# Another order at the joints of a two-layer decoder step: staggered first pair of the mixing, P1 and P2 of the third FFN unit moved ahead

## The chip, the cores and the metric

One core of one Trainium2 chip. The metric is the device time of one execution of the whole program in microseconds; lower is better. The engines named here are TensorE (PE), VectorE (DVE), ScalarE (ACT), GpSimd (POOL) and SyncE (SP), which issues the loads. Each runs its own list of instructions in order and waits on semaphores.

## What is computed

The reference is one inference step of a decoder with two layers. 512 prompt tokens and 64 sample tokens go through with the same weights, in float32; the model width is 1024, that of the feed-forward network (FFN) 2816. Per layer:

```python
x = LN1(ALPHA * x + 0.5 * swiglu(x, ffn1_w_gate, ffn1_w_up, ffn1_w_down))
h = x @ w_in                      # pool input | q | k | v | cross q | 3 branch gates
y = (causal pooling, sliding-window attention with sinks, cross-attention into 256 memory tokens)
merged = sum(sigmoid(gate_b) * (y_b @ w_br_b) for b in range(3))
x = LN2(ALPHA * x + merged @ w_o)
x = LN3(ALPHA * x + 0.5 * swiglu(x, ffn2_w_gate, ffn2_w_up, ffn2_w_down))
```

The text calls everything between LN1 and LN2 the mixing. Outputs are x and the new caches.

## The kernel before, in words

**Numbers.** x lies transposed in SBUF: eight chunks (c) of 128 channels, each with 576 tokens in two halves (h) of 288. A matmul takes 128 x 128 weights and 288 tokens. Each float32 operand is split in a rounded part and its rest ("hi" and "lo"); `mm3` does three matmuls: hi x hi, hi x lo, lo x hi. ScalarE makes the rounded parts (`fill`, `round_w`, `round_x`, `round_sums`, `round_hidden`), VectorE or GpSimd the rests (`rest_of_sum`, `rest_w`, `rest_of_x`, `rest_of_sums`, `rest_of_hidden` on VectorE; `rest_of_quarter` and half of the mixing's chunks on GpSimd).

**FFN units.** Four FFNs run in a step, numbered fb 0 to 3 (two per layer). Most of an FFN is a list of units u (gate and up columns of a 128-column block, kind "G", or part of the down product, kind "D"), each by a fast 2x2 scheme with seven products P1 to P7 instead of eight; it needs sums of weight quarters (`first_sums`, `second_sum`, `third_sum` on VectorE) and sums of x (`sums_of_x`, for the four pairs i of chunks). A product of a G unit is 12 matmuls. P1, P2 and P4 take weight quarters as they are, rounded by ScalarE and GpSimd; P5, P6, P7 and P3 take sums. P1 and P2 take x itself, P5, P6, P7, P3, P4 sums of x (only the third unit has to wait for these, pair by pair, L1764 on: `xt_lo`). P1, P6, P7 and P4 accumulate one after the other in one PSUM bank; between them ScalarE copies it out: P1's value to another bank (`copy_p1`), P6's to u2 (L768), P7's to u3 (L739).

**The head.** The first two units (g = 0, 1) are done plainly: for each half h, unit g and w (gate, up) a product of 24 matmuls, so eight of them. `silu` and `head_hidden` turn them into hidden values; `hidden_sums` adds these up to forms, `round_hidden` and `rest_of_hidden` split the forms. The head begins while the layer norm before it still works: TensorE takes chunk after chunk as it is normalised (`round_x`, `finish_x` add the bias on ScalarE). Then comes the third unit, u = 2 (`HEADS`): P1, P5, P6, P2, P7.

**Order.** Every engine's order is written out by hand. `RUN` is that of TensorE's products, `HIGH` that of ScalarE's roundings, `LOW` and `LOW_POOL` those of the rests. On ScalarE the head is followed by `ffn`, for u = 2: copy_p1, round_hidden(0, 1), fill of P1 of u = 3, P4 and P3 of u = 2, `fill_a21` of u = 3, then the copy to u2. `fill_a21(3)` (L641) waits for VectorE's `rest_of_sum(2, "P3")`, which follows `rest_of_hidden(0, 1)` there. `SLOT` gives each product its place in the weight buffers; the head's and the tail's blocks use these places by number (`HEAD_SLOT`, `TAIL_SLOT`), and `fill` of the third unit waits until the head's product that had the place is done.

**The tail and the norms.** The last part of the down product is eight products p per half (`tail`), in pairs w, each pair added to x by `tail_sums` (L1194) and, from w = 1 on, into the sum for the mean (L1198). Half 1 of the tail runs while half 0 is normalised: `mean`, `center` (L1205), squares, `variance` (L1707), root, reciprocal, `scale` (L1214), rounding, rest. After FFN 1 of a layer `norm_plain` leads to `project_first`, which does the first two 128-column blocks s = 0, 1 of w_in in pair buffers 0 and 1; it has to wait for the tail's sums of these buffers, w = 2 and 3. Half 0 goes chunk by chunk through both blocks; in half 1 block 1 lags four chunks behind. After FFN 2 of layer 0 `norm_head(0, 2)` leads to the head of FFN 1 of layer 1. Mean and variance of half 1 are put between TensorE's products of the next part.

TensorE's order for the third unit and the wait of its P7 (for G units `read` is the count of ScalarE's copies from the bank, so P7 waits for the copy of P6's result to u2):

```python
RUN += [(HEADS, p) for p in ("P1", "P5", "P6", "P2", "P7")]
...
                elif prod == "P7":
                    pe.wait_ge(read, count - 1)
```

Of the kernel before, what the change touches and what calls it, by code (L numbers as in the profile page):

```python
# [7 lines left out]
ALU = mybir.AluOpType  # L8
# [4 lines left out]
P = 128  # L13
D = 1024
KC = D // P
# [4 lines left out]
TH = T // 2  # L20
# [62 lines left out]
RUN += [(HEADS, p) for p in ("P1", "P5", "P6", "P2", "P7")]  # L83
HIGH += [(HEADS, p) for p in ("P1", "P5", "P2", "P6", "P7")]
# [80 lines left out]
def build(nc, wblk, wg, wd, wt_d, x0, mem0, cst_d, par_d, mks_d, mvs_d, kcs_d, vcs_d, sps_d,  # L165
          y_out, kT_out, v_out, poolp_out, pools_out, mk_out, mv_out, kc_out, vc_out):
    with ExitStack() as ctx:
# [414 lines left out]
        def _(act):  # L582
# [99 lines left out]

            def head(fb):
# [27 lines left out]
                silu(1, 1)  # L711
                fill(fb, HEADS, "P6")
                fill(fb, HEADS, "P7")

            def ffn(fb):
                for u in range(HEADS, FU + 1):
# [5 lines left out]

                    def copy_p1():

                        act.wait_ge(f_done, done(fb, u, "P1"))
                        act.wait_ge(ep_set, 1)
                        if old:
                            act.wait_ge(c11_silu, g_count(fb, u - 1))
                        elif u > HEADS:
                            act.wait_ge(ep_free, d_count(fb, u - 1))  # L730
                        nc.scalar.activation(ep, al[u % 2], ACT.Copy).then_inc(p1_copied, 1)
# [68 lines left out]
            def round_x(l, n, h):  # L800

                for c in range(KC):
# [3 lines left out]
                    if (h, c) == (0, 3):  # L806
                        fill_head(2 * l + n, 0, 3)

# [8 lines left out]
            def norm_plain(l):  # L817
                prime(ACT.Sqrt)
                for h in range(2):
                    square(l, 0, h)  # L820
                    root(l, 0, h)
                    for c in range(KC):
# [7 lines left out]
                        if h == 0 and c in (3, KC - 1):  # L830

                            s = c // 4
# [154 lines left out]
        def _(dve):  # L987
# [107 lines left out]
            def head(fb):  # L1095
# [3 lines left out]
                for i in range(2):  # L1099
                    sums_of_x(fb, i)  # L1100
# [15 lines left out]
                rest_of_sum(fb, HEADS, "P7")  # L1116
                rest_of_hidden(fb, 0, 1)
# [72 lines left out]
            def tail_sums(fb, w, h):  # L1190
# [4 lines left out]
                if w > 0:  # L1195
                    dve.drain()
                    acc = two(lnsum[:, :])
                    nc.vector.tensor_tensor(acc, x[:, 0:2, half(h)] if w == 1 else acc, xw, ALU.add)  # L1198
                if w == KC // 2 - 1:
                    dve.drain().then_inc(sum_ready, 1)  # L1200

# [21 lines left out]
            def norm_plain(l):  # L1223
# [15 lines left out]
                for c in range(KC):  # L1239
# [21 lines left out]
            def norm_head(l, n):  # L1261
# [30 lines left out]
                for c in range(KC):  # L1292
# [5 lines left out]
                    if n == 2 and c == 5:  # L1298
                        tail_sums(fb - 1, 2, 1)
                rest_of_x(0, KC - 1)  # L1300
                if n == 2:
                    tail_sums(fb - 1, 3, 1)
# [311 lines left out]
        def _(pe):  # L1614
# [585 lines left out]
```

## Time and profile before

| | |
|---|---|
| median of 3 runs | 2574.58 us (2572.22 to 2579.29) |
| the profiled execution | 2574.16 us, span 2572.1 us |
| instructions | 45262 |
| VectorE busy | 1646.3 us (64%) |
| ScalarE busy | 1236.4 us (48%) |
| GpSimd busy | 608.6 us (24%) |
| mean DMA rate | 86 GB/s |
| mean granted TensorE clock | 0.975 of full speed |

The busy times are unions over the span of one execution. TensorE's share stands with the other rows below. A share says how much an engine does, not who sets the end of a stretch; for that the timelines of the engines are read side by side in the stretch. The times in a timeline are microseconds from the span's start. The four heads end at about 89, 939, 1348 and 2197 us; the first pair of the mixing is at 444 to 480 and 1703 to 1739 us, and the joint of the two layers at 1278 to 1320 us.

### The profile page before, as it was taken

The numbers are of one execution on the slowest core, as the hardware profiler recorded it, in microseconds if no ns is written. First come the engines' busy times: TensorE is split into PE (matmuls) and PEld (weight loads), VectorE is DVE, ScalarE is ACT, GpSimd is POOL, SyncE is SP. The second block draws the span as 40 slices with busy tenths as digits, with TensorE's granted clock in tenths as the row PEclk, the third lists the DMA queues.
The fourth block names the chain that finished last, engine by engine and source line by source line (L and its number), as shares of the span: only waits on it lengthen the run. The fifth ranks groups of instructions, "written<-read, shape, count | busy, mean of one in ns | idle before, by whom it ended". The sixth has DMA issues, their size and how long they took to land.

```text
span 2572.1 us, 45262 instructions
## 1 busy us (share of the span) xinstructions
PE 2446.5 (95%) x17636; PEld 2379.9 (93%) x17636; DVE 1646.3 (64%) x2752; ACT 1236.4 (48%) x2487; POOL 608.6 (24%) x540
## 2 busy tenths in 40 slices
PE   7999998899999989999989999989999998999997
PEld 6899998899999889999979999979999997999997
DVE  3878776435444587777587777664443447777775
ACT  4555554334422365655456556542343226655654
POOL 1333333120000123333423333321200001333332
PEclk9999999989999999999999999989899999999999
DMA  6132223221122212222213222323122221232221
GB/s 221 62 119 83 99 89 112 67 79 50 58 81 75 83 66 85 89 93 97 99 36 114 99 99 75 107 84 107 42 55 68 80 74 66 75 107 83 94 103 54
DMA packets 53523, 220.62 MB, mean 86 GB/s; under 512 B 15521, under 2 KB 18465, under 8 KB 40225
## 3 DMA queue, kind: packets, MB, share of 16 engines
q1 hardware_dynamic: 53312, 217.74, 24.9%
q8 instruction: 142, 2.33, 0.4%
q14 instruction: 69, 0.56, 0.1%
HBM read 213.64 MB, written 6.04 MB: 85 GB/s over the span
## 4 chain that ended last, share of the span: by engine, by line
PE 80%; DVE 12%; ACT 4%; DVEq 2%; issue 1%; DMA 0%; ACTq 0%; POOL 0%
PE pair L1769 13%; PE pair L1771 12%; PE pair L1770 12%; PE pair L1618 9%; PE pair L1620 9%; PE pair L1622 9%; PE S L1769 2%; PE S L1771 2%; PE S L1770 2%; PE S L1707 2%; DVE htl L1085 2%; DVE TP L1005 1%; ACT hth L652 1%; PE S L1864 1%; PE TP L1924 1%
## 5 line engine op out<-in xcount | busy, mean ns | idle before, releaser
L1769 PE MATMUL pair<-xth,hiA 128*128 128x288 f32 x1280 | 382.4, 299 | 23.8 <-POOL loA L1532 12.5
L1770 PE MATMUL pair<-xtl,hiA 128*128 128x288 f32 x1280 | 380.9, 298 | 0.0
L1771 PE MATMUL pair<-xth,loA 128*128 128x288 f32 x1280 | 380.5, 297 | 0.0
L606 ACT ACTIVATE hiA<-TP 128x512 fp32r<-128x512 f32 (+1 forms) x384 | 200.6, 556 | 213.3 <-DVE TP L1010 141.9
L1618 PE MATMUL pair<-xh,hiA 128*128 128x288 f32 x1088 | 255.4, 312 | 26.1 <-DVE x L1194 15.8
L1532 POOL TENSOR_TENSOR loB<-rawB,hiB 128x512 fp32r<-128x512 f32 (+1 forms) x128 | 159.6, 1248 | 490.7 <-ACT hiB L606 490.7
L991 DVE TENSOR_TENSOR loA<-rawA,hiA 128x1024 fp32r<-128x1024 f32 x108 | 134.1, 1241 | 219.9 <-ACT hiA L593 219.3
L1769 PEld LDWEIGHTS pair<-xth,hiA 128*128 128x128 f32 x1280 | 242.9, 190 | 27.7 <-POOL loA L1532 13.4
L996 DVE TENSOR_TENSOR loA<-TP,hiA 128x512 fp32r<-128x512 f32 (+1 forms) x384 | 244.2, 636 | 29.6 <-ACT hiA L606 27.1
L1620 PE MATMUL pair<-xl,hiA 128*128 128x288 f32 x1088 | 244.3, 302 | 0.0
L1622 PE MATMUL pair<-xh,loA 128*128 128x288 f32 x1088 | 244.0, 302 | 0.0
L1771 PEld LDWEIGHTS pair<-xth,loA 128*128 128x128 f32 x1280 | 243.7, 190 | 0.0
L1770 PEld LDWEIGHTS pair<-xtl,hiA 128*128 128x128 f32 x1280 | 243.4, 190 | 0.0
L1532 POOL TENSOR_TENSOR loB<-rawA,hiB 128x512 fp32r<-128x512 f32 (+1 forms) x128 | 153.1, 1196 | 343.6 <-ACT hiB L606 343.6
L1618 PEld LDWEIGHTS pair<-xh,hiA 128*128 128x128 f32 x1088 | 183.2, 195 | 37.8 <-DVE loA L991 18.3
L1769 PE MATMUL pair<-xth,hiB 128*128 128x288 f32 x640 | 191.9, 300 | 14.0 <-DVE c L1142 10.1
L1770 PE MATMUL pair<-xtl,hiB 128*128 128x288 f32 x640 | 189.0, 295 | 0.0
L1771 PE MATMUL pair<-xth,loB 128*128 128x288 f32 x640 | 188.3, 294 | 0.0
L1620 PEld LDWEIGHTS pair<-xl,hiA 128*128 128x128 f32 x1088 | 183.7, 195 | 0.2
L1622 PEld LDWEIGHTS pair<-xh,loA 128*128 128x128 f32 x1088 | 182.9, 195 | 0.0
L593 ACT ACTIVATE hiA<-rawA 128x1024 fp32r<-128x1024 f32 x108 | 113.8, 1053 | 139.4 <-PE TP L1622 80.5
L1769 PE MATMUL pair<-hth,hiA 128*128 128x288 f32 x576 | 172.2, 299 | 1.7 <-DVE x L1128 1.6
(322 smaller groups left out, 6702.1 us busy)
## 6 DMA issues: line engine op xcount, KB each, us to landing
rawA<-in_wblk SPq DMA_DIRECT2D x108, 512.0 KB, 3.4
rawB<-in_wg SPq DMA_DIRECT2D x44, 1024.0 KB, 4.8
rawA<-in_wg SPq DMA_DIRECT2D x44, 1024.0 KB, 4.8
rawB<-in_wd SPq DMA_DIRECT2D x24, 768.0 KB, 4.1
rawA<-in_wd SPq DMA_DIRECT2D x24, 768.0 KB, 4.4
rawA<-in_wt_d SPq DMA_DIRECT2D x4, 1024.0 KB, 4.7
rawB<-in_wt_d SPq DMA_DIRECT2D x4, 1024.0 KB, 4.8
mcs<-in_mks SPq DMA_DIRECT2D x2, 2048.0 KB, 9.8
```

Source lines behind the costliest of these rows:

```text
L593: nc.scalar.activation(wh[:, s, :], raw[:, s, :], ACT.Copy).then_inc(w_hi, 1)
L606: nc.scalar.activation(slot((hiA, hiB), prod, n), src, ACT.Copy).then_inc(f_hi, 1)
L991: nc.vector.tensor_tensor(wl[:, s, :], raw[:, s, :], wh[:, s, :].bitcast(F32), ALU.subtract).then_inc(w_lo, 1)
L996: nc.vector.tensor_tensor(slot((loA, loB), prod, n), sum_bank(prod, n), slot((hiA, hiB), prod, n).bitcast(F32), ALU.subtract).then_inc(f_l ...
L1085: nc.vector.tensor_tensor(htl[:, n % 3, forms, :], hf[:, forms, :], hth[:, n % 3, forms, :].bitcast(F32), ALU.subtract).then_inc(h_lo, 1)
L1532: nc.gpsimd.tensor_tensor(slot((loA, loB), prod, n), quarter(u, prod, n), slot((hiA, hiB), prod, n).bitcast(F32), ALU.subtract).then_inc(f ...
L1618: nc.tensor.matmul(out(h), wt[0], xt[0](h), start=(kk == 0), stop=False)
L1620: nc.tensor.matmul(out(h), wt[0], xt[1](h), start=False, stop=False)
L1622: last = nc.tensor.matmul(out(h), wt[1], xt[0](h), start=False, stop=(kk == nk - 1))
L1769: nc.tensor.matmul(bank, wt_hi, xt[0], start=start, stop=False, skip_group_check=True)
L1770: nc.tensor.matmul(bank, wt_hi, xt[1], start=False, stop=False, skip_group_check=True)
L1771: last = nc.tensor.matmul(bank, wt_lo, xt[0], start=False, stop=i == n - 1, skip_group_check=True)
```

## The change

It changes orders and waits, and no computation.

- `RUN`: the third unit's P1 goes ahead of the head's last product; behind that come P2, P5, P6, P7. TensorE's `head` walks through `RUN` and does P1 itself. `SLOT` swaps the places of P1 and P2, so that P1's place is one that the head's first unit leaves.
- ScalarE in `head`: P1's fill moves up behind `silu(0, 1)`, then `copy_p1`, P2 and P5; `round_hidden(fb, 0, 0)` moves from behind `round_sums(1)` to the end; `round_sums(3)` moves behind P6 and P7. `finish_x` of chunks 0 to 3 is done within `round_x`.
- VectorE in `head`: `second_sum`, the rests of P6 and P7 and `third_sum` come ahead of all work on the hidden values.
- `project_first`: half 0 gets the same lag of four chunks as half 1; block 0 waits for its own weights and tail sum alone; `variance` comes behind all of half 0.
- `norm_plain` and `norm_head`: `tail_sums` is split in `tail_onto_x` (to x, which TensorE waits for) and `tail_into_mean`; the first comes earlier, the second later. `round_w` and `rest_w` of block 0 come earlier.
- The head of FFN 1 of layer 1 has mean and variance one product later, as the other heads have them.

```diff
-SLOT = {"P1": 0, "P6": 1, "P5": 2, "P7": 3, "P2": 4, "P4": 5, "P3": 6}
+SLOT = {"P2": 0, "P6": 1, "P5": 2, "P7": 3, "P1": 4, "P4": 5, "P3": 6}
-TAIL_SLOT = [(EXTRA, 0, 2, 1, 3, 4, 5, 6), (4, EXTRA, 5, 6, 0, 2, 1, 3)]
+TAIL_SLOT = [(EXTRA, 2, 1, 3, 0, 4, 5, 6), (4, EXTRA, 5, 6, 0, 2, 1, 3)]
-RUN += [(HEADS, p) for p in ("P1", "P5", "P6", "P2", "P7")]
-HIGH += [(HEADS, p) for p in ("P1", "P5", "P2", "P6", "P7")]
+RUN[-1:] = [(HEADS, "P1"), RUN[-1]] + [(HEADS, p) for p in ("P2", "P5", "P6", "P7")]
+HIGH += [(HEADS, p) for p in ("P1", "P2", "P5", "P6", "P7")]
...
@@ ScalarE, head
                 if fb:
-                    for c in range(KC):
+                    for c in range(4, KC):
                         finish_x(l, n, 1, c)
                 round_sums(fb, 0)
                 silu(0, 1)
+                fill(fb, HEADS, "P1")
                 round_sums(fb, 1)
-                round_hidden(fb, 0, 0)
+                copy_p1(fb, HEADS)
+                fill(fb, HEADS, "P2")
+                fill(fb, HEADS, "P5")
                 round_sums(fb, 2)
-                fill(fb, HEADS, "P1")
-                fill(fb, HEADS, "P5")
-                round_sums(fb, 3)
-                fill(fb, HEADS, "P2")
                 silu(1, 1)
                 fill(fb, HEADS, "P6")
                 fill(fb, HEADS, "P7")
+                round_sums(fb, 3)
+                round_hidden(fb, 0, 0)
...
@@ ScalarE, ffn
-                    if on:
-                        copy_p1()
                     if u == HEADS:
                         round_hidden(fb, 0, 1)
                     elif on:
+                        copy_p1(fb, u)
                         fill(fb, u, "P2")
...
@@ ScalarE, round_x
+                    if h == 1 and c >= 4:
+                        finish_x(l, n, 1, c - 4)
...
@@ ScalarE, norm_plain
-                        if h == 0 and c in (3, KC - 1):
-                            s = c // 4
+                        if h == 0 and c in (1, 3):
+                            s = c // 2
...
@@ VectorE, head
                 first_sums(fb, HEADS)
-                for i in range(2):
-                    sums_of_x(fb, i)
+                sums_of_x(fb, 0)
+                sums_of_x(fb, 1)
                 rest_of_sums(fb, 0)
                 sums_of_x(fb, 2)
                 head_hidden(fb, 0, 1)
-                hidden_sums(fb, 0)
                 rest_of_sums(fb, 1)
-                sums_of_x(fb, 3)
-                rest_of_hidden(fb, 0, 0)
-                rest_of_sums(fb, 2)
                 rest_of_sum(fb, HEADS, "P5")
                 second_sum(fb, HEADS)
-                rest_of_sums(fb, 3)
-                head_hidden(fb, 1, 1)
-                hidden_sums(fb, 1)
+                sums_of_x(fb, 3)
+                rest_of_sums(fb, 2)
                 rest_of_sum(fb, HEADS, "P6")
                 third_sum(fb, HEADS)
                 rest_of_sum(fb, HEADS, "P7")
+                rest_of_sums(fb, 3)
+                hidden_sums(fb, 0)
+                head_hidden(fb, 1, 1)
+                rest_of_hidden(fb, 0, 0)
+                hidden_sums(fb, 1)
                 rest_of_hidden(fb, 0, 1)
...
@@ VectorE, norm_plain (norm_head with n == 2: onto_x of pair 2 at c == 4, the rest alike)
-                    if c == 5:
-                        tail_sums(fb, 2, 1)
-                rest_w(pq(l, Q_IN), 0)
+                    if c == 3:
+                        rest_w(pq(l, Q_IN), 0)
+                        tail_onto_x(fb, 2, 1)
                 rest_of_x(0, KC - 1)
+                tail_onto_x(fb, 3, 1)
                 rest_w(pq(l, Q_IN), 1)
-                tail_sums(fb, 3, 1)
+                tail_into_mean(2, 1)
+                tail_into_mean(3, 1)
...
@@ TensorE, project_first
-                begin(qq, 0, u)
-                begin(qq, 1, u)
-                for w in range(2, 4):
-                    pe.wait_ge(tail_add, tail_count(2 * l, w, 1))
...
+                for h in range(2):
+                    turns = [(c, 0) for c in range(lag)] + [(c - lag * s, s) for c in range(lag, KC) for s in range(2)]
+                    for c, s in turns + [(c, 1) for c in range(KC - lag, KC)]:
+                        if h == 0 and c == 0:
+                            begin(qq, s, u)
+                            pe.wait_ge(tail_add, tail_count(2 * l, 2 + s, 1))
...
-                    if (h, c, s) == (0, 6, 1):
+                        if (h, c, s) == (0, KC - 1, 1):
...
@@ TensorE, head
+                for _, g, w, h in [what for what in RUN if what[0] == "H"]:
...
+                    if (g, w, h) == (1, 1, 1):
+                        product(fb, HEADS, "P1")
...
+                        if fb and (h, c) == (0, 3) and (g, w) == (0, 1):
+                            mean(l, n, 1)
+                        if fb and (h, c) == (0, 3) and (g, w) == (1, 0):
+                            variance(l, n, 1)
```

## Rows read from the trace of the kernel before

**Rows 1.** the page, part 1: engine, busy us, share of span, instructions

```profile
PE 2446.5 (95%) x17636; PEld 2379.9 (93%) x17636; DVE 1646.3 (64%) x2752; ACT 1236.4 (48%) x2487; POOL 608.6 (24%) x540
```

**Rows 2.** waits of TensorE, 905 to 945 us: us, times, longest

```profile
PE pair L1769 <- POOL loA L1532: 3.6, 1, 3.6
PE pair L1769 <- DVE loA L996: 1.2, 1, 1.2
```

**Rows 3.** timeline of VectorE, 912 to 939 us: start, us, instruction

```profile
913.88 1.23 DVE L1005 TENSOR_TENSOR TP<-S,rawA 128x1024 f32<-128x1024 f32 x1
...
921.92 0.46 DVE L1032 TENSOR_TENSOR tf<-x,tf 128x288 f32<-128x288 f32 x1
...
926.38 1.36 DVE L1032 TENSOR_TENSOR tf<-x,tf 128x288 f32<-128x288 f32 x1
...
929.80 0.68 DVE L996 TENSOR_TENSOR loA<-TP,hiA 128x512 fp32r<-128x512 f32 x1
...
932.27 0.45 DVE L1092 SCALAR_TENSOR_TENSOR hf<-c,pair 128x288 f32<-128x288 f32 x1
...
933.63 0.46 DVE L1076 TENSOR_TENSOR hf<-hf 128x288 f32<-128x288 f32 x1
934.01 0.68 DVE L996 TENSOR_TENSOR loA<-TP,hiA 128x512 fp32r<-128x512 f32 x1
...
935.81 1.65 DVE L1085 TENSOR_TENSOR htl<-hf,hth 128x1440 fp32r<-128x1440 f32 x1
...
938.78 1.23 DVE L1005 TENSOR_TENSOR TP<-S,rawB 128x1024 f32<-128x1024 f32 x1 [0.73 <-ACT S L641]
```

**Rows 4.** timeline of ScalarE, 912 to 942 us

```profile
913.77 3.50 ACT L814 ACTIVATE x<-x,par 128x288 f32<-128x288 f32 x8
...
923.62 0.68 ACT L652 ACTIVATE hth<-hf 128x576 fp32r<-128x576 f32 x1 [3.46 <-DVE hf L1071]
...
934.13 1.41 ACT L652 ACTIVATE hth<-hf 128x1440 fp32r<-128x1440 f32 x1 [1.55 <-DVE hf L1076]
...
938.15 0.60 ACT L641 ACTIVATE S<-rawB 128x512 f32<-128x512 f32 x1 [1.09 <-DVE loB L996]
938.69 0.39 ACT L768 ACTIVATE u<-pair 128x288 f32<-128x288 f32 x1
```

**Rows 5.** timeline of TensorE, 923 to 940 us

```profile
927.48 0.61 PE L1769 MATMUL pair<-xth,hiA 128*128 128x288 f32 x1 [3.60 <-POOL loA L1532]
...
939.18 0.37 PE L1769 MATMUL pair<-xth,hiA 128*128 128x288 f32 x1 [0.98 <-issue]
```

**Rows 6.** timeline of GpSimd, 912 to 942 us

```profile
925.95 1.48 POOL L1532 TENSOR_TENSOR loA<-rawA,hiA 128x512 fp32r<-128x512 f32 x1 [21.09 <-ACT hiA L606]
929.57 1.45 POOL L1532 TENSOR_TENSOR loB<-rawA,hiB 128x512 fp32r<-128x512 f32 x1 [2.14 <-ACT hiB L606]
```

**Rows 7.** windows: length, busy us per engine, granted clock, DMA share

```profile
448.35:455.18 6.83, 3.19 (x13) 3.21 (x14) 4.04 (x5) 1.47 (x3) 0.97 (x1) 0.50 0.50 156
926.22:933.05 6.83, 5.57 (x22) 5.42 (x23) 6.54 (x9) 3.51 (x7) 2.66 (x2) 0.50 0.00 0
```

**Rows 8.** timeline of TensorE, 440 to 480 us

```profile
452.00 0.58 PE L1618 MATMUL pair<-xh,hiA 128*128 128x288 f32 x1 [7.89 <-DVE x L1194]
```

**Rows 9.** timeline of VectorE, 434 to 455 us

```profile
442.40 0.94 DVE L1214 SCALAR_TENSOR_TENSOR x<-x,par,lnstd 128x288 f32<-128x288 f32 x2
...
449.85 1.22 DVE L991 TENSOR_TENSOR loA<-rawA,hiA 128x1024 fp32r<-128x1024 f32 x1
451.00 0.75 DVE L1194 TENSOR_TENSOR x<-x,pair 128x576 f32<-128x576 f32 x1
```

**Rows 10.** timeline of VectorE, 1286 to 1306 us

```profile
1295.98 0.74 DVE L1194 TENSOR_TENSOR x<-x,pair 128x576 f32<-128x576 f32 x1
...
1303.90 2.27 DVE L1205 TENSOR_TENSOR x<-x,TP 128x288 f32<-128x288 f32 x6 [2.41 <-PE TP L1700]
```

More of the change, by code:

```diff
@@ L681, in prime, with copy_p1 @@
                 nc.scalar.activation(small[:, 60:61], small[:, 61:62], function)
+            def copy_p1(fb, u):
+                act.wait_ge(f_done, done(fb, u, "P1"))
+                act.wait_ge(ep_set, 1)
+                if u > HEADS:
+                    if SEQ[u - 1][0] == "G":
+                        act.wait_ge(c11_silu, g_count(fb, u - 1))
+                    else:
+                        act.wait_ge(ep_free, d_count(fb, u - 1))
+                nc.scalar.activation(ep, al[u % 2], ACT.Copy).then_inc(p1_copied, 1)
             def head(fb):
@@ L721, in ffn @@
                     groups = H_GROUPS[j_old // 2] if old else []
[L723 to L731, printed above, removed]
                     def fill_next(prod):
@@ L1188, in ffn, with tail_onto_x @@
                     tail_sums(fb, w, 0)
-            def tail_sums(fb, w, h):
+            def tail_onto_x(fb, w, h):
                 dve.wait_ge(f_done, done(fb, "T", 2 * w + 1, h))
@@ L1194, in tail_sums, with tail_into_mean @@
                 nc.vector.tensor_tensor(xw, xw, halves(pair[w % 2]), ALU.add).then_inc(tail_add, 1)
[L1195 to L1198, printed above, removed]
+            def tail_into_mean(w, h):
+                dve.drain()
+                acc = two(lnsum[:, :])
+                nc.vector.tensor_tensor(acc, x[:, 0:2, half(h)] if w == 1 else acc, x[:, 2 * w:2 * w + 2, half(h)], ALU.add)
                 if w == KC // 2 - 1:
                     dve.drain().then_inc(sum_ready, 1)
+            def tail_sums(fb, w, h):
+                tail_onto_x(fb, w, h)
+                if w > 0:
+                    tail_into_mean(w, h)
             def center(l, n, h):
@@ L1297, in norm_head @@
                         tail_sums(fb - 1, 1, 1)
-                    if n == 2 and c == 5:
-                        tail_sums(fb - 1, 2, 1)
+                    if n == 2 and c == 4:
+                        tail_onto_x(fb - 1, 2, 1)
                 rest_of_x(0, KC - 1)
                 if n == 2:
-                    tail_sums(fb - 1, 3, 1)
+                    tail_onto_x(fb - 1, 3, 1)
+                    tail_into_mean(2, 1)
+                    tail_into_mean(3, 1)
                 else:
@@ new lines, in head @@
+                l, n = ((fb - 1) // 2, 2 - f) if fb else (None, None)
+                for _, g, w, h in [what for what in RUN if what[0] == "H"]:
+                    if h == 1:
+                        pe.wait_ge(head_out if w else head_silu, head_count(fb, g, 0))
+                    elif f == 1 and g == 1:
+                        pe.wait_ge(pair_free[w], n_use(fb // 2, Q_WO + 3) + 2)
+                    elif f == 0 and fb > 0:
+                        pe.wait_ge(tail_add, tail_count(fb - 1, 2 + w, 1))
+                    if (g, w, h) == (1, 1, 1):
+                        product(fb, HEADS, "P1")
+                    for c in range(KC):
+                        q_no = 2 * w + c % 2
+                        if h == 0 and c < 2:
+                            pe.wait_ge(f_lo_p, lo_p_count(fb, "H", g, q_no))
+                        if g == 0 and w == 0:
+                            pe.wait_ge(xf_lo, x_count(fb, h, c))
+                        cols = slice(c // 2 * P, c // 2 * P + P)
+                        last = mm3(lambda _: (al, de)[w][g], [head_slot(f, part, g, q_no)[:, cols] for part in range(2)],
+                                   [lambda _, t=t: x_form(t, h, c) for t in ((xth, xbh), (xtl, xbl))], c, KC, (h,))
+                        if fb and (h, c) == (0, 3) and (g, w) == (0, 1):
+                            mean(l, n, 1)
+                        if fb and (h, c) == (0, 3) and (g, w) == (1, 0):
+                            variance(l, n, 1)
+                    last.then_inc(f_done, 1)
@@ L1834, in ffn @@
                 for what in RUN:
-                    if what[0] not in ("H", "T"):
+                    if what[0] not in ("H", "T") and what != (HEADS, "P1"):
                         product(fb, *what)
```

45 lines of the change are left out of this document (8 added, 37 removed).

## The prediction

> **What bounds the kernel now.** I read the page first: the matmul row is busy 95% of the span [rows 1], so there is little to win, and only where TensorE stands still. TensorE's waits over a head's end (905 to 945 us) name 3.6 us for GpSimd's rounding of the third unit's P1 and 1.2 us for VectorE's rounding of a sum [rows 2]; a third, 0.98 us, ends at P7 [rows 5]. "Third unit" is u = 2, HEADS. Is it really those products that set the end of this stretch? VectorE's timeline says no. From `first_sums` at 913.88 on it is never idle for longer than a drain until the rounding of P3 is done: the first real idle is the 0.73 us before 938.78, so 24.2 us, to 938.05, are without a hole [rows 3]. ScalarE goes on from there: a21 of the next unit at 938.15, then the copy of P6's result (u2, L768) at 938.69 [rows 4], and P7, which accumulates on the same bank, starts at 939.18 [rows 5]. So a head ends when a VectorE chain ends, 25.3 us after `first_sums`; the 3.6 us of idle TensorE lies beside that chain and costs nothing. After P7 TensorE runs without such a stop. The program has four heads of this form.
>
> **Step 1, the head (four times).** P1 goes ahead of the head's last product and P2 ahead of P5. That moves 2 x 12 matmuls to an earlier place and removes none. It can gain only if VectorE's chain gets shorter. Its operations are the same, in another order, so I look for the idle that the order makes.
> (a) Before, between `hidden_sums(1)` (its last operation starts at 933.63) and the rounding of its result (935.81) VectorE does three operations (P6's rounding, the third sum, P7's rounding), which fill the 1.80 us from 934.01 on [rows 3]. They cover ScalarE's `round_hidden(0, 1)`, 1.41 us from 934.13 [rows 4]. After, these three stand ahead of `hidden_sums(0)`, and nothing lies between: VectorE waits the 1.41 us and a handing over of some 0.07. The same happens once more, smaller, at `round_hidden(0, 0)`: 0.68 us [rows 4], of which `head_hidden(1, 1)`, 0.45 at 932.27 [rows 3], hides a part: 0.37 stay, with hand-overs. Sum 1.85 us. `fill(3, "P1")`, P4, P3, a21 and the u2 copy are all queued on ScalarE behind `round_hidden(0, 1)`, and P7 behind them, as before.
> (b) `finish_x` of chunks 0 to 3 moves in between the rounds of x. Eight of them take 3.50 us now [rows 4], 0.43 each; three fit into ScalarE's holes between the rounds of x, which follow VectorE's pace, and the last one stands ahead of `silu(1, 0)` and a21, for which `first_sums` waits: 0.4 us later. Not in head 0, which has no such step. That ScalarE is 1.7 us freer afterwards gains nothing, since its `round_sums(0)` waits for VectorE's sums.
> (c) GpSimd's roundings of P1 and P2, and VectorE. Before, P1's at 925.95 met VectorE's L1032 at 926.38, which took 1.36 us instead of the 0.46 of the same line at 921.92; P2's at 929.57 met one that reads PSUM (929.80), which took no more than its like at 934.01, 0.68 [rows 3, 6]. After, P1's weights are rounded at about 919.4 and P2's at 923.6, both among the sums of x, which are SBUF only: two delays of 0.9 against one, +0.9.
> On this the Trainium skill (SBUF — State Buffer, § SBUF: two separate sides) is sterner: a VectorE operation with two SBUF inputs and a GpSimd one that reads SBUF shut each other out for the whole instruction. By that rule each of the two delays could be the whole 1.45 us of such a rounding, and the sum below would be 4 x 1.1 higher, 2596.0 us. The rows agree that the second waits, but the 0.9 is what this trace shows of it.
> Sum: 1.85 + 0.9 = 2.75 in head 0, 3.15 in the other three: 12.2 us. Bounds for a head: 1.5 (a alone, the smaller part hidden) and 4.0 (P1 rounded late, so that the last product too stands behind it).
>
> **Step 2, TensorE's clock behind the head.** A matmul took 3.19 / 13 = 0.245 us at the low level [rows 7], so some 0.13 at the high one: 1.6 us for a product of 12, 3.2 for one of the head's 24, 0.39 for a turn of three. P1, the last product and P2 now follow each other (6.4 us); then P5 needs rounded sums 3 and 4 of x, which VectorE gives at about 931.2 and 934.3. P6 ends at about 936.5, and P7 starts at 939.18 + 3.15 = 942.3: some 6 us of idle TensorE at the very end of the chain, where 0.98 were [rows 5]. After 7.9 us of idle before 452.00 the granted clock was 0.50, the 1.2 GHz level, from 448.35 to 455.18, so 3.2 us of it fell on work; after 3.6 us before 927.48 it was 0.50 until 933.05, 5.6 us of it on work [rows 5, 7, 8]. That second one costs nothing now, since VectorE's chain is longer. After the change the low level reaches past P7, where TensorE is the bound: half of the mean of 3.2 and 5.6 is 2.2 us, four times 8.8. Bounds: 0 (the level stays, as a shorter idle might allow), and half of the whole 6.83, 3.4, per head.
>
> **Step 3, the first pair of the mixing (two layers).** TensorE starts at 452.00 after 7.9 us of idle, when the last tail sum has been added (VectorE, 451.00 to 451.75) [rows 8, 9]. After, block 0 needs only its own weights and the third pair sum: rest_w(0) moves up behind chunk 2 (442.4, where the scales of chunks 4 and 5 now start, + 1.22, its duration at 449.85) [rows 9], `tail_onto_x(2, 1)` ends at about 444.4, and TensorE runs five turns, to 446.5. Then block 1's weights come: VectorE does four scales, two rests, the last `onto`, then rest_w(1): about 451.0. So 4.9 us of idle are left of 7.9. But the remaining turns now run at 0.50 for longer: before, 3.19 us of work fell on the low level [rows 7]; now a low stretch that begins some 3 us later takes in up to 6.8, 1.8 us lost; and the last two turns (0.8 us) come ahead of the variance instead of behind it. 3.0 - 1.8 - 0.8 = 0.4. If the stretch begins where it did, 2 us. I take 1.0 per layer, 2.0 together. Bounds: 0 and 4.6 (mean 3.1 us earlier and both low stretches gone). The sums `into` the mean follow rest_w(1) and end at 452.8, before TensorE reaches the mean; the earlier round_w(0) on ScalarE stands in its wait for chunk 2 and delays nobody. SP's loads have their waits unchanged.
>
> **Step 4, the joint of the two layers (once).** The pair sum that TensorE waits for is added from 1295.98 to 1296.72 [rows 10]; it moves to about 1294.2, behind chunk 4. Mean comes one product later but without its low clock: the centring, now at 1303.90 [rows 10], would start at 1302.4, and the variance chain ends about 1.6 us earlier. From there the head of step 1 follows: 1.6 us gained. Bounds 0 and 3.2.
> Slots of P1 and P2 swap numbers; each has its slot to itself within the units, and the tail's fills wait for products long done: nothing. The last norm is untouched.
>
> **The sum.** 12.2 + 8.8 - 2.0 - 1.6 = +17.4 us. The profiled execution took 2574.16 us with a span of 2572.1, against a median of 2574.58 (2572.22 to 2579.29), so it stands for the median within 0.5 us. 2574.2 + 17.4 = 2591.6. A measurement can tell 0.3%, 7.7 us: faster is below 2566.5, slower above 2582.
>
> **Rivals.**
> A. TensorE is the bound at the heads after all (faster). Mechanism: in the joint of the mixing, work put into the idle keeps the clock at 2.4 GHz and each layer's joint gives 4.6 us; in the heads the new holes on VectorE are covered by something I take as waiting. Point of decision: P7 of unit 2 starts no later than 25.3 us after `first_sums`. For it: TensorE did wait 3.6 us for P1 and 8 us for the tail sum. Against: VectorE without a hole. 2574.2 - 9.2 - 1.6 = 2563.4. Chance 0.14.
> B. The heads lose their 12.2 us, but the clock stays up past P7, and the other joints give all, 9.2 + 1.6: 2574.2 + 12.2 - 10.8 = 2575.6, no change that can be told. For: five turns in the hole at 444. Against: every idle of over 3 us read above was followed by 0.50. Chance 0.18.
> C. The change doesn't do what it says: P1's weights are late although asked for sooner, because ScalarE reaches the fill only behind `round_sums(0)` and `silu(0, 1)`, and GpSimd then waits for VectorE; P1 holds up the ready last product, and copy_p1 holds ScalarE's P2 and P5. 1.3 us more per head: 2591.6 + 5.2 = 2596.8. Chance 0.08.
> The forecast has 0.60. Its own range, by the bounds, is 2580 to 2604. The range for all goes from 2567 (into A's side) to 2603. Slower: C and nearly all of the forecast, 0.64; within 0.3%: B and the forecast's lower edge, 0.22; faster: A, 0.14.
>
> **What would show it.** In the changed trace: P7 (L1769, the first write of the pair bank after P6) starts 27.5 to 29 us after `first_sums` (25.3 before); VectorE idles some 1.5 us ahead of its 128x1440 rounding, waiting for ScalarE; P5 shows two stops for the rounded sums; the granted clock is 0.50 behind P7. In the mixing's joint: TensorE starts within 1 us of the tail's end, stops some 4.5 us for rest_w, and the mean comes about 1 us earlier. I am wrong if VectorE is idle less than 1 us between `first_sums` and P3's rounding, or if P7 follows P6 closely.

## The result, and the profile after

The changed kernel takes 2588.75 us (median of 5 runs, 2584.64 to 2590.36); the kernel before, run beside it, takes 2574.13 us (2571.70 to 2579.29). The ratio is 1.0052, with a 95% interval of 1.004 to 1.0064: slower by 0.52%, 13.4 us. The forecast was 2591.6 us. The profiled execution of the changed kernel took 2589.03 us with a span of 2587.0, so it stands for the median within 0.3 us, and can be compared with the forecast step by step.

Part 1 of the page has the same work in a span that is 14.9 us longer; only TensorE's busy time grew [rows 1], by 12.5 us for the same 17636 matmuls, and that is a slower clock, not more work:

```profile
PE 2459.0 (95%) x17636; PEld 2387.4 (92%) x17636; DVE 1646.4 (64%) x2752; ACT 1236.8 (48%) x2487; POOL 609.2 (24%) x540
```

**The head.** The waits of TensorE from 905 to 945 us no longer name GpSimd's rounding of P1 [rows 2]. The wait that the change was made against is gone, and another stands there:

```profile
PE pair L1780 <- DVE xtl L1041: 5.2, 2, 2.8
PE pair L1780 <- issue: 4.4, 2, 4.3
```

VectorE's timeline, which had no hole of over 0.2 us between `first_sums` and the rounding of P3 [rows 3], now has two, each ahead of a rest of hidden values and each ended by ScalarE's rounding of them (L652):

```profile
914.66 1.23 DVE L1008 TENSOR_TENSOR TP<-S,rawA 128x1024 f32<-128x1024 f32 x1
...
919.83 2.50 DVE L1041 TENSOR_TENSOR xtl<-tf,xth 128x1152 fp32r<-128x1152 f32 x1
...
924.88 1.81 DVE L1041 TENSOR_TENSOR xtl<-tf,xth 128x1152 fp32r<-128x1152 f32 x1
...
935.72 0.76 DVE L1088 TENSOR_TENSOR htl<-hf,hth 128x576 fp32r<-128x576 f32 x1 [0.39 <-ACT hth L652]
936.57 0.76 DVE L1077 TENSOR_TENSOR hf<-hf 128x576 f32<-128x576 f32 x1
937.40 0.46 DVE L1079 TENSOR_TENSOR hf<-hf 128x288 f32<-128x288 f32 x1
939.33 1.66 DVE L1088 TENSOR_TENSOR htl<-hf,hth 128x1440 fp32r<-128x1440 f32 x1 [1.47 <-ACT hth L652]
```

The holes are 0.39 and 1.47 us. ScalarE's rows are those of before [rows 4], only later: the rounding, a21, and the copy to u2, behind which P7 stands:

```profile
937.89 1.40 ACT L652 ACTIVATE hth<-hf 128x1440 fp32r<-128x1440 f32 x1 [2.21 <-DVE hf L1079]
...
941.68 0.60 ACT L641 ACTIVATE S<-rawB 128x512 f32<-128x512 f32 x1 [0.86 <-DVE loB L999]
942.22 0.39 ACT L769 ACTIVATE u<-pair 128x288 f32<-128x288 f32 x1
```

GpSimd's two roundings [rows 6] came forward. The first now begins together with VectorE's L1041 of 919.83:

```profile
919.82 1.29 POOL L1546 TENSOR_TENSOR loB<-rawA,hiB 128x512 fp32r<-128x512 f32 x1 [14.59 <-ACT hiB L606]
924.09 1.39 POOL L1546 TENSOR_TENSOR loA<-rawA,hiA 128x512 fp32r<-128x512 f32 x1 [2.97 <-ACT hiA L606]
```

TensorE's timeline has the two stops within P5, and then P7, 28.05 us after `first_sums` where it was 25.30 [rows 3, 5]:

```profile
927.67 0.29 PE L1780 MATMUL pair<-xth,hiA 128*128 128x288 f32 x1
...
931.41 0.41 PE L1780 MATMUL pair<-xth,hiA 128*128 128x288 f32 x1 [2.78 <-DVE xtl L1041]
...
934.47 0.61 PE L1780 MATMUL pair<-xth,hiA 128*128 128x288 f32 x1 [2.39 <-DVE xtl L1041]
...
942.71 0.58 PE L1780 MATMUL pair<-xth,hiA 128*128 128x288 f32 x1 [4.27 <-issue]
943.09 0.45 PE L1781 MATMUL pair<-xtl,hiA 128*128 128x288 f32 x1
943.33 0.45 PE L1782 MATMUL pair<-xth,loA 128*128 128x288 f32 x1
```

The last two rows start 0.24 us apart where a matmul at full clock takes 0.13: TensorE runs at the 1.2 GHz level behind P7. The granted clock in these windows shows it: the first lies in the mixing's first pair and answers to [rows 7], the second ahead of P7, the third at P7. (Behind the window and its length stand the busy us of TensorE, its weight loads, VectorE, ScalarE and GpSimd, then granted clock, DMA share and GB/s.)

```profile
454.20:461.00 6.80, 6.16 (x21) 5.59 (x22) 2.33 (x4) 0.00 (x0) 0.00 (x0) 0.50 0.25 77
...
932.10:938.90 6.80, 3.97 (x15) 3.62 (x15) 5.12 (x8) 1.69 (x2) 0.00 (x0) 0.50 0.00 0
942.30:945.70 3.40, 2.99 (x12) 3.02 (x13) 2.52 (x3) 1.21 (x3) 1.04 (x1) 0.50 0.41 82
```

**The mixing's first pair.** In TensorE's timeline the wait of 7.89 us [rows 8] has become one of 0.43 and one of 3.72, with five turns of three matmuls between them:

```profile
448.90 0.37 PE L1632 MATMUL pair<-xh,hiA 128*128 128x288 f32 x1 [0.43 <-DVE x L1197]
...
454.84 0.61 PE L1632 MATMUL pair<-xh,hiA 128*128 128x288 f32 x1 [3.72 <-DVE loA L994]
```

**Where the 14.9 us are.** I took the start of the same operations in both traces (P7 of each head, the mean and variance of each norm, the first product behind the first pair) and looked where the difference grows. In us:

| stretch | grows by (negative: shorter) | forecast |
|---|---|---|
| four heads, up to P7 | 2.55 + 2.18 + 2.80 + 2.28 = 9.8 | 12.2 |
| from P7 to the next mean (clock) | 1.86 + 1.33 + 2.66 + 2.76 = 8.6 | 8.8 |
| mixing, first pair, layers 0 and 1 | -1.91 - 3.58 = -5.5 | -2.0 |
| joint of the two layers | -2.33 | -1.6 |
| stretches that the diff doesn't touch | -1.15 + 2.5 + 2.96 = +4.3 | 0 |

The last line is two attention parts and the last norm. Their work is the same; low stretches of the clock lie elsewhere in them. From the last mean to the end it is 38.4 us here, with a granted clock of 0.50 from 2567.1 to 2573.9, and 35.4 both before and in the trace of the changed joints alone. So a single trace can carry some 3 us of this that no part of the diff explains. That is why each part was run by itself.

### The profile page after: what moved, and what is told of

Its sections match the earlier page's. It is cut to its first block, busy times and chain, and to the rows that moved or that the text cites. A ratio compares the mean times of both kernels' runs of the same rounds, so it can differ in the third digit from the quotient of the medians.

```text
span 2587.0 us, 45262 instructions
## 1 busy us (share of the span) xinstructions
PE 2459.0 (95%) x17636; PEld 2387.4 (92%) x17636; DVE 1646.4 (64%) x2752; ACT 1236.8 (48%) x2487; POOL 609.2 (24%) x540
## 3 DMA queue, kind: packets, MB, share of 16 engines
q8 instruction: 142, 2.33, 0.4%
## 4 chain that ended last, share of the span: by engine, by line
PE 79%; DVE 12%; ACT 5%; DVEq 2%; issue 1%; DMA 0%; POOL 0%; ACTq 0%
PE pair L1780 12%; PE pair L1782 12%; PE pair L1781 12%; PE pair L1632 9%; PE pair L1634 9%; PE pair L1636 9%; PE S L1718 2%; DVE htl L1088 2%; PE S L1780 2%; PE S L1782 2%; PE S L1781 2%; ACT hth L652 2%; DVE TP L1008 1%; PE S L1875 1%; PE TP L1935 1%
## 5 line engine op out<-in xcount | busy, mean ns | idle before, releaser
L1780 PE MATMUL pair<-xth,hiA 128*128 128x288 f32 x960 | 290.4, 303 | 35.2 <-DVE xtl L1041 17.9
L1780 PE MATMUL pair<-xth,hiB 128*128 128x288 f32 x960 | 287.5, 300 | 14.7 <-DVE c L1145 10.9
L1781 PE MATMUL pair<-xtl,hiA 128*128 128x288 f32 x960 | 288.9, 301 | 0.0
L1782 PE MATMUL pair<-xth,loA 128*128 128x288 f32 x960 | 288.2, 300 | 0.0
L1781 PE MATMUL pair<-xtl,hiB 128*128 128x288 f32 x960 | 284.6, 296 | 0.0
L1782 PE MATMUL pair<-xth,loB 128*128 128x288 f32 x960 | 283.9, 296 | 0.0
L1780 PEld LDWEIGHTS pair<-xth,hiA 128*128 128x128 f32 x960 | 185.0, 193 | 38.4 <-DVE xtl L1041 20.0
L1780 PEld LDWEIGHTS pair<-xth,hiB 128*128 128x128 f32 x960 | 181.6, 189 | 22.1 <-issue 20.4
L1546 POOL TENSOR_TENSOR loA<-rawB,hiA 128x512 fp32r<-128x512 f32 (+1 forms) x64 | 76.4, 1194 | 497.1 <-ACT hiA L606 497.1
L1782 PEld LDWEIGHTS pair<-xth,loB 128*128 128x128 f32 x960 | 181.9, 190 | 0.0
L1781 PEld LDWEIGHTS pair<-xtl,hiB 128*128 128x128 f32 x960 | 181.7, 189 | 0.0
## 6 DMA issues: line engine op xcount, KB each, us to landing
mcs<-in_mks SPq DMA_DIRECT2D x2, 2048.0 KB, 10.1
```

Source lines behind the costliest of these rows:

```text
L1546: nc.gpsimd.tensor_tensor(slot((loA, loB), prod, n), quarter(u, prod, n), slot((hiA, hiB), prod, n).bitcast(F32), ALU.subtract).then_inc(f ...
L1780: nc.tensor.matmul(bank, wt_hi, xt[0], start=start, stop=False, skip_group_check=True)
L1781: nc.tensor.matmul(bank, wt_hi, xt[1], start=False, stop=False, skip_group_check=True)
L1782: last = nc.tensor.matmul(bank, wt_lo, xt[0], start=False, stop=i == n - 1, skip_group_check=True)
```

## The experiments

Two sets, each timed against the kernel before on the same chip: the first four against a median of 2576.52 us, the last four against 2574.38 us.

### One half of the change at a time

`joints_only` has the heads of before (order, `SLOT`, ScalarE's and VectorE's `head`) and all the changed joints; `heads_only` is the other way round.

```diff
 joints_only, against the changed kernel
-RUN[-1:] = [(HEADS, "P1"), RUN[-1]] + [(HEADS, p) for p in ("P2", "P5", "P6", "P7")]
+RUN += [(HEADS, p) for p in ("P1", "P5", "P6", "P2", "P7")]
 heads_only, against the changed kernel
-                        if h == 0 and c in (1, 3):
-                            s = c // 2
+                        if h == 0 and c in (3, KC - 1):
+                            s = c // 4
...
```

> The changed joints (first pair of the mixing, joint of the two layers) on the heads of before. The forecast's steps 3 and 4 say 3.6 us faster than before (2570.5); the trace of the changed kernel, read against that of before, says some 6 (2568). Rival B says 9.2 + 1.6 = 10.8 us faster (2563). If the joints are worth nothing it is 2574.

> The changed heads on the joints of before. Forecast: steps 1 and 2, 12.2 + 8.8 = 21 us slower than before (2595), P7 of the third unit 28.05 us after first_sums in all heads. If only the longer chain of VectorE counts and the low clock behind it costs nothing: 12 us slower (2586). If TensorE is the bound at the heads (rival A): no slower than before.

Measured: joints_only 2567.23 us, ratio 0.9963 (0.995 to 0.9975); heads_only 2595.95 us, ratio 1.0077 (1.0063 to 1.0091). Against their shared before that is -9.3 and +19.4 us. So the change is a gain and a loss twice as large, added up (10.1 us, and 13.4 for the whole change, which the intervals allow). The heads cost what Steps 1 and 2 say (12.2 + 8.8 = 21.0; the interval is 16 to 23). The joints give more than the 3.6 of Steps 3 and 4; even the near end of the interval is 6.4.

In heads_only the hole and P7 are where they are in the changed kernel, P7 28.06 us after `first_sums` (919.76); in joints_only P7 comes after 25.6 to 26.3 us, near the 25.3 to 26.0 of the kernel before. VectorE's and TensorE's timelines of heads_only:

```profile
942.51 0.46 DVE L1079 TENSOR_TENSOR hf<-hf 128x288 f32<-128x288 f32 x1
944.44 1.66 DVE L1088 TENSOR_TENSOR htl<-hf,hth 128x1440 fp32r<-128x1440 f32 x1 [1.47 <-ACT hth L652]
```

```profile
947.82 0.58 PE L1772 MATMUL pair<-xth,hiA 128*128 128x288 f32 x1 [4.41 <-issue]
```

### Is it the clock behind the head?

`warm_heads` is the changed kernel with matmuls that nothing reads in TensorE's three waits of each head: 7 and 6 at the stops of P5, 15 ahead of P7 (these 15 take 5.84 us).

```diff
+            def warm(n):
+                for _ in range(n):
+                    nc.tensor.matmul(pair[1][:, 0, 288:512], ident, cst[:, 0:224], start=False, stop=True, skip_group_check=True)
...
+                if (u, prod) == (HEADS, "P7"):
+                    warm(15)
...
+                    if (u, prod) == (HEADS, "P5") and i >= 2:
+                        warm(9 - i)
```

> The changed kernel, with dummy matmuls of TensorE (identity times a constant into unused columns of P5's bank) where it stands still for P5's third and fourth pair and for P7: 7, 6 and 15 in each head. They keep the engine busy and wait for nothing; the outputs are the same. If the low clock behind the wait is a cost of its own (step 2), it goes: about 8.8 us faster than the changed kernel (2580), with P7 still 28.05 us behind first_sums and a granted clock of 1.0 behind it. If the low clock costs nothing, or the chain alone makes the loss: the same as the changed kernel, 2588.8. If the dummies hold up the real work, slower than it.

Measured: 2580.63 us, ratio 1.0018 (1.0008 to 1.0027), 8.7 us below the changed kernel's ratio. P7 starts 28.91, 27.83, 28.05 and 28.06 us after `first_sums` in the four heads, 0.45 us later in sum than in the changed kernel; in heads 0 and 1 it follows the unread matmuls without a wait. So what is gained is the clock. Windows over two heads, first of the changed kernel, then of warm_heads:

```profile
930.00:950.00 20.00, 11.93 (x63) 11.38 (x64) 14.76 (x20) 10.03 (x17) 4.91 (x4) 0.74 0.17 54
1340.00:1360.00 20.00, 11.64 (x50) 11.09 (x51) 14.73 (x20) 8.81 (x15) 3.44 (x2) 0.66 0.16 53
```

```profile
930.00:950.00 20.00, 20.00 (x131) 20.00 (x130) 14.66 (x23) 9.95 (x18) 6.92 (x5) 1.00 0.15 54
1340.00:1360.00 20.00, 19.43 (x125) 18.76 (x125) 15.14 (x23) 10.33 (x19) 7.04 (x5) 1.00 0.15 54
```

The 0.74 and 0.66 have become 1.00. From P7 to the next mean the four heads together take 8.6 us more than in the kernel before in the trace of the changed kernel, 9.2 in that of heads_only, and 0.6 in that of warm_heads. So Step 2's 8.8 us are shown as a cause, not only as a sum. A loss in VectorE's chain alone would have left the time where it was.

### Cover ScalarE's rounding again

`cover_round` keeps the changed head and gives VectorE back what lay behind each rounding: P6's rest behind `head_hidden(1, 1)`, the third sum and P7's rest behind `hidden_sums(1)`.

```diff
-                rest_of_sum(fb, HEADS, "P6")
-                third_sum(fb, HEADS)
-                rest_of_sum(fb, HEADS, "P7")
...
                 head_hidden(fb, 1, 1)
+                rest_of_sum(fb, HEADS, "P6")
                 rest_of_hidden(fb, 0, 0)
                 hidden_sums(fb, 1)
+                third_sum(fb, HEADS)
+                rest_of_sum(fb, HEADS, "P7")
                 rest_of_hidden(fb, 0, 1)
```

> The changed kernel, with VectorE's rounding of P6 put over ScalarE's round_hidden(0, 0), and third_sum and P7's rounding behind hidden_sums(1), over round_hidden(0, 1), where they stood before. Step 1a says that VectorE's two holes (0.39 and 1.47 us) are closed to some 0.3: the chain from first_sums to P7 goes from 28.05 to 26.5 us, 4 x 1.5 = 6 us faster than the changed kernel (2583). Rival: the loss comes from GpSimd and VectorE shutting each other out and from P1's place, then nothing moves.

Measured: 2581.36 us, ratio 1.002 (1.0011 to 1.0029). VectorE's timeline: the hole of 0.39 is gone, that of 1.47 is 0.27.

```profile
933.84 0.75 DVE L1088 TENSOR_TENSOR htl<-hf,hth 128x576 fp32r<-128x576 f32 x1
...
935.89 0.69 DVE L1018 TENSOR_TENSOR S<-rawA,TP 128x512 f32<-128x512 f32 x1
936.49 0.68 DVE L999 TENSOR_TENSOR loA<-TP,hiA 128x512 fp32r<-128x512 f32 x1
937.44 1.66 DVE L1088 TENSOR_TENSOR htl<-hf,hth 128x1440 fp32r<-128x1440 f32 x1 [0.27 <-ACT hth L652]
```

P7 follows `first_sums` by 26.60, 25.66, 26.38 and 26.38 us, where it was 28.27, 28.05, 28.04 and 28.04: 7.4 us sooner in all, and the ratio fell by 0.0032, 8.2 us. The holes are 1.59 us shorter, and in three heads P7 is 1.66 or 1.67 sooner: a hole of VectorE in the head is paid one for one, as (a) of Step 1 says. The further 0.7 us of head 1 come from the meeting of VectorE and GpSimd, which the next run brings up.

### The bias of x in its old place

`no_finish` takes `finish_x` of chunks 0 to 3 out of `round_x` again.

```diff
-                    for c in range(4, KC):
+                    for c in range(KC):
                         finish_x(l, n, 1, c)
...
-                    if h == 1 and c >= 4:
-                        finish_x(l, n, 1, c - 4)
```

> The changed kernel, with finish_x of chunks 0 to 3 behind silu(1, 0) and a21 again, not within round_x. Step 1b says 0.4 us a head in the three heads that have it: first_sums follows the reciprocal of its norm 0.4 us sooner, 1.2 us faster than the changed kernel in all, which is within the noise of the runs but can be read in the trace. Rival: sums_of_x then has to wait for finish_x and the gain is lost.

Measured: 2584.32 us, ratio 1.0035 (1.0023 to 1.0047), 4.4 us below the changed kernel; the two intervals overlap a little. The timeline of VectorE has `first_sums` (L1006) 0.79 us behind the start of the last rest of x, where the changed kernel has 1.20 and the kernel before 0.80: (b) of Step 1 is exactly its 0.4. But in these heads 1 to 3 P7, too, comes 27.33 or 27.34 us after `first_sums`, 0.7 sooner than the 28.05 of the changed kernel, which (b) alone would have left as it was. VectorE, then GpSimd, of no_finish:

```profile
914.72 0.52 DVE L1289 SCALAR_TENSOR_TENSOR xtl<-x,par,xth 128x288 fp32r<-128x288 f32 x1 [0.17 <-ACT xth L805]
...
915.51 1.23 DVE L1006 TENSOR_TENSOR TP<-S,rawA 128x1024 f32<-128x1024 f32 x1
...
920.67 1.36 DVE L1039 TENSOR_TENSOR xtl<-tf,xth 128x1152 fp32r<-128x1152 f32 x1
922.12 1.35 DVE L1028 TENSOR_TENSOR tf<-x 128x288 f32<-128x288 f32 x1
```

```profile
920.86 2.30 POOL L1544 TENSOR_TENSOR loB<-rawA,hiB 128x512 fp32r<-128x512 f32 x1 [14.37 <-ACT hiB L606]
```

Here VectorE's L1039 began 0.19 us before GpSimd's rounding, and GpSimd paid (2.30 for 1.29) while VectorE kept its 1.36 and lost 0.9 only in the next operation (1.35, where 0.45 is usual). In the changed kernel both began within 0.01 us, and VectorE paid there (2.50) and once more later (1.81), 1.6 in all. The 0.4 us of (b) move these two against each other, so that (b) and (c) are not independent, as I had them.

But the outcome can change without any edit. In head 1 of warm_heads and of cover_round, where VectorE's, ScalarE's and GpSimd's orders up to here are those of the changed kernel, GpSimd again begins 0.01 us ahead or at the same time, and this time GpSimd paid. ScalarE's copy to u2 came 0.7 us sooner behind `first_sums` for it than in heads 2 and 3. VectorE's rows and GpSimd's of warm_heads:

```profile
919.31 1.36 DVE L1041 TENSOR_TENSOR xtl<-tf,xth 128x1152 fp32r<-128x1152 f32 x1
920.76 1.34 DVE L1030 TENSOR_TENSOR tf<-x 128x288 f32<-128x288 f32 x1
919.30 2.48 POOL L1546 TENSOR_TENSOR loB<-rawA,hiB 128x512 fp32r<-128x512 f32 x1 [14.60 <-ACT hiB L606]
```

### The mixing alone

`mixing_only` is the kernel before with the first pair staggered: `project_first`, `rest_w` and `round_w` of block 0 earlier, `tail_sums` split in `norm_plain`.

```diff
                     if c == 3:
+                        rest_w(pq(l, Q_IN), 0)
+                        tail_onto_x(fb, 2, 1)
...
```

> Of the changed joints only the first pair of the mixing (two places); the joint of the two layers and the heads are those of before. Both joints together gave some 8 us. Step 3 says 1.0 us a layer (0 to 4.6), step 4 1.6 for the joint of the layers. If the traces of the changed kernel tell the shares rightly (1.9 and 3.6 us in the two layers, 1.6 at the joint of the layers), this one is 5.5 us faster than before, and joints_only 2 to 3 us faster still. If step 3 is right, only 2 us faster.

Measured: 2570.06 us, ratio 0.9983 (0.9974 to 0.9992), -4.4 us, where Step 3 says -2.0. By the same landmarks the first pair gives 3.4 us in layer 0 and 2.5 in layer 1 in this trace, 1.9 and 3.6 in that of the changed kernel: 2.9 in the mean. The other traces agree. From the mean to the first product behind the pair the old order takes 51.8 to 52.3 us (before and heads_only), the new one 48.4 to 49.9 (the seven traces that have it without unread matmuls in it), 2.9 less in the mean. The stops are the same in all of these seven. TensorE's timeline of mixing_only:

```profile
444.86 0.37 PE L1627 MATMUL pair<-xh,hiA 128*128 128x288 f32 x1 [0.44 <-DVE x L1194]
...
450.80 0.61 PE L1627 MATMUL pair<-xh,hiA 128*128 128x288 f32 x1 [3.72 <-DVE loA L991]
...
465.92 0.61 PE L1627 MATMUL pair<-xh,hiA 128*128 128x288 f32 x1 [4.30 <-DVE xl L1238]
```

### An earlier copy to u2

`u2_early` is joints_only with ScalarE's copy of P6's result put ahead of a21 of the next unit.

```diff
+                    if u == HEADS:
+                        act.wait_ge(f_done, done(fb, u, "P6"))
+                        nc.scalar.activation(u2[:, :], al[u % 2], ACT.Copy).then_inc(al_act, 1)
...
-                    if g:
+                    if g and u > HEADS:
```

> joints_only, with ScalarE's copy of P6's result to u2 ahead of fill_a21(3) in the third unit, so that P7 no longer hangs on VectorE's chain. If that queue place is what sets the end of a head, P7 starts some 1.1 us earlier behind first_sums (24.0 instead of 25.2), as soon as P2 is done, and the program is 2 to 4 us faster than joints_only (some 0.95 a head as far as the copy to u3 lets P4 start). If VectorE's chain binds TensorE at P3 or at the next unit anyway, P7 moves and the program does not get faster.

Measured: 2566.32 us, ratio 0.9967 (0.9955 to 0.998), against 0.9963 of joints_only: no gain that these intervals can tell. In the traces P7 starts 1.4 and 1.1 us sooner behind `first_sums` in heads 3 and 2, but not in heads 0 and 1 (26.2 and 25.9 us, where joints_only has 26.3 and 25.7): there it follows P2 without a wait in either run. In head 2, the only one where it waited in joints_only, it waits no more and starts 24.54 us after `first_sums` instead of 25.65. TensorE's timeline, joints_only and then u2_early:

```profile
1343.43 0.37 PE L1777 MATMUL pair<-xth,hiA 128*128 128x288 f32 x1 [0.97 <-issue]
...
1370.98 0.37 PE L1777 MATMUL pair<-xth,hiB 128*128 128x288 f32 x1 [0.15 <-DVE c L1142]
```

```profile
1341.79 0.29 PE L1780 MATMUL pair<-xth,hiA 128*128 128x288 f32 x1
...
1370.18 0.37 PE L1780 MATMUL pair<-xth,hiB 128*128 128x288 f32 x1 [0.84 <-DVE c L1145]
```

Of the 0.97 us that P7 no longer waits, 0.69 come back as a longer wait for VectorE one unit later. From `first_sums` to the next mean the four heads take 1459.1 us in joints_only and 1458.6 in u2_early. P7 is a landmark of VectorE's chain, and moving it without shortening the chain brought next to nothing.

### A version that beats both

`best` is u2_early with unread matmuls in the remaining waits of the joints, as in warm_heads: 9 and 11 at the two stops of the mixing's first pair, 5 ahead of the head of each FFN 2, 5 and 3 in the last norm.

```diff
+                        if (h, c, s) == (0, 0, 1):
+                            warm(pair[0][:, 0, :], 9)
+                        if (h, c, s) == (1, 0, 0):
+                            warm(pair[0][:, 0, :], 11)
...
```

> u2_early with dummy matmuls in TensorE's waits at the joints, as in warm_heads: 9 and 11 in the first pair of the mixing (ahead of block 1 of half 0 and ahead of half 1), 5 ahead of the head of FFN 2, 5 and 3 in the last norm. If the low clock behind these waits costs as it did in the heads (2.1 us each), the two of the mixing give 3 to 5 us over both layers, the head of FFN 2 up to 3, the last norm up to 3 in the executions that meet the low level there: 5 to 8 us faster than u2_early, and less spread. If the low clock lies beside VectorE's and ScalarE's work there, nothing.

Measured: 2563.85 us, ratio 0.9952 (0.994 to 0.9965): 10.5 us faster than the kernel before, some 25 faster than the changed one. The windows over the two first pairs have a clock of 1.00 (joints_only, over its own two pairs: 0.84 and 0.80), and the pairs take 30.4 and 30.5 us where joints_only took 31.9 and 33.1:

```profile
444.00:475.00 31.00, 27.35 (x157) 24.25 (x158) 21.26 (x38) 16.83 (x33) 9.87 (x13) 1.00 0.11 36
1696.00:1727.00 31.00, 27.45 (x158) 24.35 (x159) 21.15 (x39) 16.95 (x33) 9.87 (x13) 1.00 0.12 36
```

That would be 4.1 us; the median is 2.5 below that of u2_early, with intervals that overlap. That it beats the kernel before is shown, that the unread matmuls are worth 4 us here is not.

## Why the prediction was right, step by step

**What bounds the head.** Right where it matters: giving VectorE's chain two holes moved P7 by them, and closing them moved it back (cover_round). But I had read one head for all, and in the kernel before TensorE was close behind. In its head 3 the copy to u2 began at 2195.75, as early behind `first_sums` as in head 1, yet P7 started only at 2196.96, right behind P2 and without a wait: the clock had been at 0.50 from 2185.7 to 2195.9. In joints_only that is so in three of the four heads. There TensorE, slowed by its clock, set the start of P7, by 0.3 to 1.0 us.

**Step 1 (a).** Forecast 1.85 us of idle, measured 0.39 + 1.47 = 1.86, at the two places named.

**Step 1 (b).** Forecast 0.4 in three heads: measured 0.40 (1.20 or 1.21 for 0.80), and 0.79 again when it is undone.

**Step 1 (c).** In heads 1 to 3 the count of two delays against one was right, their size a little off: 1.14 (2.50 for 1.36) and 0.46 (1.81 for 1.35), against one of 0.90, so +0.7 where I took +0.9. With 0.2 of hand-overs head 1 comes to the 2.75 that P7 moved. In head 0 (c) failed: VectorE was delayed once, by 0.93 (1.38 for 0.45), as before. In its place stands a wait that I did not have. `copy_p1` waits for TensorE's P1 until 74.06 (10.7 us behind `first_sums`, in head 1 8.4), ScalarE's rounding for P5 stands behind it, and VectorE is idle for 0.84 us. Over the four heads P7 moved by 2.97, 2.75, 2.39 and 2.03 from `first_sums`, 10.1 where 4 x 2.75 = 11.0 was taken: heads 2 and 3 were slower before (25.65 and 26.01). The table has 9.8, although (b) should add 0.4 in three heads. The clock made up for that on the way to `first_sums`; a low stretch at 885 us, for example, lasted 10.2 us before and 6.8 after. And (c) is not independent of (b), by no_finish. On the exclusion that the Trainium skill states (SBUF — State Buffer, § SBUF: two separate sides) the rows now say more than those of before: the one that comes second waits for nearly all that is left of the other. In four cases shown where VectorE came second (one before, two in the changed kernel, one in no_finish), GpSimd's rounding had 1.05, 1.28, 0.60 and 1.04 us left, and VectorE lost 0.90, 1.14, 0.46 and 0.90, each 0.14 or 0.15 less. So the traces agree with the rule that one of the two waits, but the price is what is left of the other instruction, not the whole of it twice; the 2596.0 that two whole ones gave was too much.

**Step 2.** Forecast 8.8, measured 8.6 between P7 and the next mean, and 8.7 by the ratio of warm_heads. The single heads (1.3 to 2.8) scatter with how much of the low stretch falls behind P7: 4.2, 3.0, 5.5 and 5.9 us of matmuls, where 4.4 was taken for each. The idle itself was misread. Of the 6 us in one piece ahead of P7 only 4.27 are there, since an earlier low stretch, 932.1 to 938.9, slowed P5 and P6, which ended later for it. That costs nothing, because P7 waits anyway.

**Step 3.** This is the term that was mis-sized: -2.0 forecast, -4.4 by mixing_only and -5.5 in the trace of the changed kernel. The stops were nearly right (4.9 us of idle left; the waits are 0.43 and 3.72, the starts 0.73 and 4.02 apart, 4.75). So was the variance's place, two turns (0.8) later. What failed is the clock. I let the low stretch behind the stop take up to 1.8 us in each layer, and of the two outcomes that this left, 0.4 and 2, took 1.0. I had compared with one low stretch of the kernel before, which met 3.19 us of matmuls. With the old order it meets 3.2 and 3.8 us of them before and 4.7 and 5.4 in heads_only; with the new order 3.0 to 6.2 in the seven traces, 4.5 in the mean against 4.3. Half of the difference is 0.1 us lost, not 1.8. 3.15 - 0.8 - 0.1 = 2.25 per layer, where the traces have 2.9. Of the rest, 0.3 lies at the end of the pair. From the second stop to the next product it takes 10.7 us in every trace but that of the kernel before, which has 11.4 in both layers. But heads_only has the old order and 10.7 too (1743.58 to 1754.32), so this part is not shown to come from the change. The last 0.3 stays open. The forecast's and the measured size both lie within the bounds that I gave.

**Step 4.** Forecast -1.6, measured -2.3 in the traces of the changed kernel and of joints_only.

**The sum.** 17.4 forecast; the profiled executions differ by 14.9, the medians by 14.6, the ratio says 13.4. The heads were taken 2.6 us too high and the joints 4.2 us too low; 4.3 us in stretches that nothing touched bring it back near the forecast. The agreement of the total with 2591.6 is thus partly luck; that of Step 2 and of (a) and (b) is not, while (c) had the wrong mechanism in one head of four. The forecast's own range was misnamed, too: its upper end, 2604, follows from the bounds of the steps, but their lower bounds add up to 2567.8, not 2580.

**The rivals.** A: P7 comes later than 25.3 us, so it falls; but its second half, joints that give much, is near the truth (joints_only -9.3 against A's -10.8). B has the joints nearly right and the clock behind the head wrong. warm_heads takes the low clock out as B assumes, and its 2580.63 lies between B's 2575.6 and the forecast's 2591.6. C: P1 is not late. In head 1 it starts at 921.22, and the last product follows it without a stop at 922.88. So C falls as a forecast; but its second half, `copy_p1` holding up ScalarE, did happen in head 0 and cost VectorE the 0.84 us named under (c).

## What to carry to other kernels

Before an operation is moved ahead of others, write down what it was covering: here three short VectorE operations stood between a sum and its use, and hid a rounding of ScalarE that then cost its full length. A long wait of the busiest engine need not be the bound; ask whose chain has no hole, and count only what shortens that chain. And price an idle of TensorE twice, once as time and once as the slow clock on the work behind it; compare with several low stretches of the kernel before, not with one, as they differ from place to place. When a change helps in one place and hurts in another, run the two halves apart.

## What was not expected of the hardware

- Which of VectorE and GpSimd pays when they meet in SBUF turned on 0.2 us or less. Starting 0.19 us ahead of GpSimd, VectorE took its usual 1.36 us and GpSimd 2.30 instead of 1.29. Starting within 0.01 us of it, VectorE took 2.50 in the changed kernel (heads 1 to 3), but 1.36 in head 1 of warm_heads and cover_round, where GpSimd took 2.48. What decides this stays open.
- The clock's low stretches move from place to place in parts of the program that no edit touches: the last mean to the end took 38.4 us in the trace of the changed kernel, 37.2 and 37.1 in those of warm_heads and u2_early, and 35.4 to 35.6 in the other seven. In the first three a low stretch (6.8, 3.4 and 3.4 us) falls on the last norm. What decides its place stays open, too.
